# Constant matrix products placed in the waits of TensorE inside the norms of a four-layer network

## The reference

```
def rms_norm(x, gain=None):
    y = xf * lax.rsqrt(jnp.mean(xf * xf, axis=-1, keepdims=True) + RMS_EPS)
...
    # layers 0 and 1, both halves
    h = rms_norm(x, norm_g[l, 0]) * (1.0 + sc1) + sh1
    y = mixer_block(h, ...)
    x = x + gt1 * rms_norm(y, norm_g[l, 1])
...
    # layers 2 and 3, both halves
    h = rms_norm_2(x, norm_mix[l]) * (1 + sc_m) + sh_m
    x = x + gt_m * y
```

## Time and profile before

| | |
|---|---|
| median of three timed runs | 1566.22 us |
| the profiled execution | 1564.95 us, span 1563.2 us |
| mean granted TensorE clock over the span | 0.953 |
| PE busy | 1494.6 us (96%) |
| DVE busy | 1090.8 us (70%) |
| ACT busy | 751.6 us (48%) |
| PE's products L543 and L848 in the chain that ended last | 51% and 14% of the span |

### The profile page before, as it was taken

The page is one execution under the profiler, slowest core; times in us unless marked ns, Lnnn a source line. Parts: engine busy times, 40 slices in busy tenths (PEclk is TensorE's granted clock), DMA queues, the critical chain, the costliest instruction groups (busy, mean ns, idle before and its releaser), DMA issues.

```text
span 1563.2 us, 28157 instructions
## 1 busy us (share of the span) xinstructions
PE 1494.6 (96%) x12014; PEld 1469.9 (94%) x12014; DVE 1090.8 (70%) x1469; ACT 751.6 (48%) x1019; POOL 406.2 (26%) x391
## 2 busy tenths in 40 slices
PE   3999899999899999999899899999999999999998
PEld 3999899999899999999899889999999999999998
DVE  7877697798456587799675666766468667465544
ACT  3546355434546455534577345444354344454432
POOL 0123020496120120297000311200429412220022
PEclk7998799999899989999799998999989999999999
DMA  9773469797252449799243014877537665456640
GB/s 393 314 293 118 173 261 347 287 343 285 84 195 101 154 179 362 291 341 341 89 182 108 1 57 162 297 295 270 189 137 295 217 240 208 170 190 216 223 181 28
DMA packets 47211, 336.69 MB, mean 215 GB/s; under 512 B 5360, under 2 KB 5744, under 8 KB 6768
## 3 DMA queue, kind: packets, MB, share of 16 engines
q1 hardware_dynamic: 46224, 333.03, 57.0%
q10 hardware_dynamic: 864, 1.87, 0.3%
HBM read 333.83 MB, written 1.05 MB: 214 GB/s over the span
## 4 chain that ended last, share of the span: by engine, by line
PE 83%; POOL 9%; DVE 4%; issue 2%; ACT 1%; DMA 1%; POOLq 0%; ACTq 0%; DVEq 0%
PE PS L543 51%; PE PS L848 14%; POOL acts_hi_lo L770 4%; POOL acts_hi_lo L772 4%; PE PS L615 3%; PE PS L787 3%; PE PS L1087 1%; PE PS L623 1%; DVE ring L449 1%; DMA arena<-in_x_dram 1%; PE PS L2049 1%; PE PS L2386 1%; PE PS L1473 1%; PE PS L2064 1%; DVE spare L670 1%
## 5 line engine op out<-in xcount | busy, mean ns | idle before, releaser
L438 DVE TENSOR_TENSOR weights_hi_lo<-ring,weights_hi_lo 128x1024 fp32r<-128x1024 f32 x426 | 551.3, 1318 | 271.2 <-ACT weights_hi_lo L429 270.0
L429 ACT ACTIVATE weights_hi_lo<-ring 128x1024 fp32r<-128x1024 f32 x426 | 444.6, 1058 | 475.3 <-PE PS L543 271.0
L543 PE MATMUL PS<-hi,weights_hi_lo 128*128 128x256 f32 x3456 | 561.8, 285 | 14.8 <-ACT hi L659 12.1
L543 PEld LDWEIGHTS PS<-hi,weights_hi_lo 128*128 128x128 f32 x3456 | 480.2, 193 | 18.1 <-issue 14.5
L848 PE MATMUL PS<-acts_hi_lo,weights_hi_lo 128*128 128x256 f32 x3168 | 376.9, 281 | 1.3 <-DVE weights_hi_lo L438 1.1
L848 PEld LDWEIGHTS PS<-acts_hi_lo,weights_hi_lo 128*128 128x128 f32 x3168 | 375.6, 188 | 2.0 <-issue 1.3
L543 PE MATMUL PS<-lo,weights_hi_lo 128*128 128x256 f32 x1728 | 349.2, 284 | 0.0
L770 POOL CAST acts_hi_lo<-arena 128x256 fp32r<-128x256 f32 x142 | 132.6, 934 | 806.0 <-PE PS L848 438.7
L543 PEld LDWEIGHTS PS<-lo,weights_hi_lo 128*128 128x128 f32 x1728 | 270.3, 192 | 0.0
L449 DVE CUSTOM_DVE_ANT_0 ring<-ring,cond 128x1024 f32<-128x1024 f32 x192 | 253.3, 1358 | 0.0
L772 POOL TENSOR_TENSOR acts_hi_lo<-arena,acts_hi_lo 128x256 fp32r<-128x256 f32 x142 | 170.1, 1198 | 11.4
(11 more groups left out here) (362 smaller groups left out, 1123.3 us busy)
## 6 DMA issues: line engine op xcount, KB each, us to landing
ring<-in_stream_dram SPq DMA_DIRECT2D x313, 1024.0 KB, 4.9
constS<-in_const_dram SPq DMA_DIRECT2D x1, 1856.0 KB, 8.7
cond<-in_rows_dram SPq DMA_DIRECT2D x2, 512.0 KB, 5.2
arena<-in_x_dram ACTq DMA_DIRECT2D x1, 1024.0 KB, 11.2
smallS<-in_small_dram SPq DMA_DIRECT2D x1, 883.0 KB, 13.0
out_dram<-arena ACTq DMA_DIRECT2D x2, 256.0 KB, 2.5
out_dram<-arena SPq DMA_DIRECT2D x2, 256.0 KB, 2.9
constS<-in_const_dram SPq DMA_DIRECT2D x1, 320.0 KB, 14.3
```

What stands on the lines that cost most here:

```text
L429: act.activation(wsp[:, g % 2, 0, at:at + HALF], ring[:, n % RING, at:at + HALF], ACT.Copy).then_inc(*ready.one())
L438: dve.tensor_tensor(wsp[:, g % 2, 1, at:at + HALF], ring[:, n % RING, at:at + HALF], wsp[:, g % 2, 0, at:at + HALF].bitcast(F32), ALU.subt ...
L543: mm = pe.matmul(o, lhs, rhs, start=k + g + j == 0, stop=k == KD - 1 and j == 2, skip_group_check=True)
```

## The change

A constant array `idle` (128 x 512, float32r) is filled once at the start by two ACT copies from the constants. For that, ACT now waits for positions and constants to have landed, makes the two copies, and only then goes on to the wait for `cond` and the issue of x's load.

PE multiplies this array by itself, into PSUM banks that nothing reads, at these places:

- y norm of layers 0 and 1: 5 products of 128 columns between the sums and the spread, 9 of 512 columns behind the spread;
- x norm at all seven seams (not in the first norm): 5 products of 128 columns behind each of the first three units' sums, 2 of 512 columns behind the last unit's sums, 4 of 512 columns behind the spread.

No wait and no semaphore is added on PE, and the sums and the spreads themselves stay as they were.

```diff
+        idle = sb("idle", [P, 512], F32R)
...
+        def idle_products(pe, n, bank, width):
+
+            for _ in range(n):
+                pe.matmul(PS[:, bank, 0:width], idle[:, 0:P], idle[:, 0:width], start=True, stop=True)
+
...
-        def norm_of(l, half, updated):
+        def norm_of(l, half, updated, filled):
...
                 for u in range(len(UNITS)):
                     unit_sums(pe, u, sq, 0, xsq, xsum)
+                    if filled and u < 3:
+                        idle_products(pe, 5, filled[0], P)
+                if filled:
+                    idle_products(pe, 2, filled[0], 512)
                 spread(pe, r, 2, xr, rx)
+                if filled:
+                    idle_products(pe, 4, filled[1], 512)
...
-            norm = norm_of(0, 0, xt)
+            norm = norm_of(0, 0, xt, None)
...
                 act.dma_start(smallS[:, 0:early_small], small[:, 0:early_small]).then_inc(*biases.dma())
+                act.wait_ge(*inp.at(32))
+                for i in range(2):
+                    act.activation(idle[:, 256 * i:256 * i + 256], constS[:, 0:256], ACT.Copy)
                 act.wait_ge(*cond_in.at(16))
...
-            norm = norm_of(*next_norm, xu) if next_norm else None
+            norm = norm_of(*next_norm, xu, (2, 3) if 2 not in y_banks else (5, 6)) if next_norm else None
...
                         unit_sums(pe, u, sq_last, 0, ysq, ysum)
+                    idle_products(pe, 5, 2, P)
                     spread(pe, r, 3, yr, ry)
+                    idle_products(pe, 9, 2, 512)
                 if norm:
                     norm[0](pe)
```

## The result

The changed kernel takes 1578.37 us (median of nine runs, 1571.19 to 1584.38) against 1567.49 us for the kernel before in the same rounds (nine runs, 1562.4 to 1571.13): ratio 1.0070, 95% interval 1.0054 to 1.0085. It is slower, by 8.5 to 13.3 us. The forecast was +11.4 us and 1577. Measured again later, the same kernel gave 1.0045 (1.0029 to 1.0062), so the two intervals together say +4.5 to +13 us. The profiled execution took 1573.45 us, the second shortest of the nine; its span is 1571.6 us, 8.4 above that of before.

A forecast was written before the change was run, and what follows sets the result against it. PE, busy for 96% of the span, was taken as the bound, at half clock behind each dense product. Terms 1.5 + 2.8 + 7.1 = +11.4 us gave 1576.4 on the profiled execution, 1577 from the median; range 1560 to 1588.

The forecast's parts named there:

- start +1.5: At the start: x's load issued at about 10.0 instead of 4.55 lands 1 to 2 us late; +1.5 us (0.3 to 4).
- first four seams +2.8: Out 0, down 0, out 1, down 1: added products cost +0.7 us each (-2.3 to +5.4), four seams +2.8.
- last three +7.1: Out 2, down 2, out 3: no wait to fill, narrow products paid in full; +2.4 us each (+0.1 to +3.5).
- The prices: On PE: a 128-column product takes 0.12 us at full clock, 0.22 at half; nine of 512 columns 3.85 at half.
- the rival of the dear product: All seven seams: 128-column products cost 0.24 us and hold the clock; sum +7 us, 1572 to 1573; chance 0.15.
- Fallen seams: Seams where the clock falls to half during the x sums: +2.2 us at each of the first four, +3.5 last three.
- the 0.5 us given back: First four seams, clock fallen: PE meets the second slot's split, hiding the four products behind the spread; -0.5 us.
- Held seams: Seams where the clock stays at 1.00: -2.3 us at each of the first four, +0.1 at the last three.
- the -0.5 for the spread: Last three seams, clock held: the x spread at full clock is 0.5 us shorter.
- The -0.7 of the first slot: Last three seams: the dense product's first slot ends 0.7 us earlier, meeting the second slot's split.
- Two seams in three: All seven seams: the clock was taken to fall at two in three, giving +0.7 us and +2.4 us a seam.
- The rival of the held clock: Clock holds at all seven seams: 4 x -2.3 + 3 x 0.1 + 1.5 = -7.4 us, 1558; chance 0.17.

## Why the prediction was right, and where it was not

**The sign, the size and the order of the terms held.** Forecast +11.4: start +1.5, first four seams +2.8, last three +7.1. Found in the profiles: start +1.7 to +2.2. Last three: 618.3, 618.1 and 617.4 us with the changed kernel's products against 609.6 to 612.9 in the five profiles with none there, +6.2 by the means. First four: the three ways without the variable one are 3 us shorter in the first profile (605.5 against 608.7), and 1 to 2 longer in the second (609.7) and in those with the load in its old place (610.7) and with none at the last three (610.3). Sum some +5 to +10. In the profiled execution the +8.4 are +1 for the start, -3 and +6 for the ways, and +4 from the way that varies. Of that, the seam down 0 is 0.7; the rest is not the change's, as the start alone has it too (164.4). That the medians came out near +11.4 is partly luck, as the parts below show.

**The prices.** 0.12 and 0.22 us for a narrow product became 0.113 and 0.214 from start to start (five in 0.61 and 1.17). The two ends of the range, 0.06 and 0.24, are out, and with them the rival of the dear product: what the nearest rows had in common decided it. The wide one is 0.231 and 0.427, inside 0.22 to 0.24 and 0.43. The Trainium skill's page "TensorE: Matmul & The Clock Gate", section "Back-to-back issue gap", has about 81 ns for 128 columns in a stream of loads and products; for float32r, of which it does not speak, these traces have 113, and the measurement decides.

**Fallen seams.** The forecast had +2.2 for each of the first four, which is +2.7 to the split, as the 0.5 us given back lie behind it. Measured to the split, from unrounded times: +1.3, +0.7 and, in the second profile, +2.0, +1.2, +0.9 and +0.5; with the load in its old place +2.1, +1.6, +1.4 and +1.3. So this term was about twice too large. The mechanism is as described (the chain at out 0 above: two units at full clock, then half), but the wide products in front of it did not always come late: at out 0 of the first profile the first x sum starts at 189.20, 5.5 us behind the dense product's last one as before, because in that execution the clock was still up during the nine. I had the fall behind the y sums in every fallen case, and it took place in only some. Windows at out 0 in the second profile show the case that I had: half clock for 3.3 us from 187.3, full again under the wide products, half again from 194.2. For the last three: +3.2, +3.6, +2.9 and +3.9, and +3.0 and +3.1 with the load in its old place, forecast +3.5 (+4.2 to the split); the values at out 3 (+3.6, +3.9, +3.1) are from its good case before. The 0.5 us given back behind the split was read at one seam and carried to four. In the trace of before, PE comes out of the first slot 0.5 us after the split at out 0 and 0.9 at down 1, but at down 0 and out 1 it already waited for it, and there nothing could be given back. The reading that the split stands 8.6 us behind the spread's end, whatever PE's clock is, holds at six of the seven seams in all twelve profiles (8.66 to 8.74 us); at down 0 it is 11.0.

**Held seams.** Forecast -2.3 for the first four (-1.8 to the split), found -2.1 and -1.4 there; with two wide products a unit -2.4 at out 0. For the last three I had +0.1 (+0.8 to the split); the held ones are +1.2 and +0.9, and +0.9 with the load in its old place. The term that was mis-sized is the -0.5 for the spread: the clock held through the sums but fell behind them, so that the spread was at half clock after all (1.05 us from its first pass at down 2), and the two wide products in front of it cost instead of fitting the wait. The -0.7 of the first slot was there: PE stood and waited for DVE's split, 0.5 to 1.2 us at these seams, where before it had come 0.7 to 0.9 us behind it.

**Two seams in three.** Four of seven fell in the sums in the first profile, six of seven in the second. With the load in its old place it was six of seven, and without products at the last three all of the first four: 20 of 25 together, more than two in three. It was a judgement between two rows. At the first four seams, where a fallen one cost about half of what was forecast but 14 of 16 fell, the two errors nearly cancel, and that is luck.

**The rival of the held clock** (-7.4 us) has the clock hold at all seven seams, and no version did that. The one with 256 columns, at the same price, came nearest with five of seven, and its time was that of the kernel before. The forecast's own terms say so too: three held and one fallen of the first four, two held and one fallen of the last three and the start make +0.5 us, against +0.8 by the ratio. Whether seven of seven would have been faster stays open. It was right that a busy PE does not hold the clock: in the changed kernel PE was busy for 10.2 of 10.2 us at half clock. The same page of the Trainium skill, section "Why this matters for your kernels", asks to avoid idle gaps. Here PE shows none in the x sums, and the clock fell in them.

**The start.** +1.5 forecast; x landed 1.6 us late. The path was other than I had it: the table load came before ACT's wait, not behind it, so x's load went out at 7.82 and not at 10.0, before even the first copy had ended. A second table load did come, and was covered. With an issue at 7.82, 3 us before the small parameters land, the forecast's account (x stood behind them until 10.8 and took 5 us from there) would have x land in time. So the 1.6 us came out right by luck. By 10.8 us ACT's queue had moved 0.48 MB in the kernel before and 0.30 in the changed one, and positions, constants and small parameters are 0.29 of it: before, 0.19 MB of x were across by then, now next to none. What is not shown is that the medians feel it: the run with the start alone leaves -1.1 to +2.8 us.

## What to carry to other kernels

A product that only keeps an engine's clock can be worth its price where the engine waits. Where the engine is itself the bound, as PE is in the last three x norms, it is added to the path in full, and the held clock must pay for it; no version here gained at those three seams. Before choosing the filler, look for its cheapest form: in float32r 128 columns cost nearly what 256 do, and two products of 512 columns bring more columns (1024 against 640) in less time (0.57 us against 0.61) than five narrow ones. Where the clock falls in other places from one execution to the next, read each part from the timelines of several profiles and leave the sum to the medians.

## What the runs showed of the hardware

- A float32r product of 128 columns with its own weight load follows the last by 0.113 us at full clock and 0.214 at half, one of 256 columns by 0.119 and 0.214, one of 512 by 0.231 and 0.427.
- Half clock came while PE was shown busy without a gap (10.2 of 10.2 us), with one-column sums and 128-column products in turn, and the clock fell in these sums at 20 of 25 seams; with 256 columns in place of 128 it stayed at full clock through the sums at five seams of seven.
- The same program had its half-clock stretches at other seams in two executions (3.4 and 9.9 us at out 1, 10 and some 3 at out 2).
- A load of 1 MB issued 3.27 us later landed 1.6 us later (9.6 us after its issue in place of 11.2). Why it made up half of the delay is not shown.
